# Slots of an expert dealt over the partitions, another order for one load back, and an earlier reload of x, in a two-layer decoder step

## The reference

```python
h = rmsnorm(x, norm_ffn[layer])
g_sel = argmax(h @ w_group + b_group)                 # one of 4 groups
top_v, top_i = top_k((h @ w_router + b_router)[g_sel], 2)   # two of its 8 experts
gates = softmax(top_v) * p_group
x = x + sum_over_the_two( gate * (silu(h @ w_gate[e]) * (h @ w_up[e])) @ w_down[e] )
```

```text
layer 0: 23 36 24 29 42 44 48 50 36 41 39 35 44 52 23 50 49 28 28 37 30 33 31 34 37 35 22 32 39 36 36 29
layer 1: 45 38 41 31 31 32 40 32 36 44 42 35 43 27 38 33 36 35 33 35 39 43 46 31 30 38 37 36 28 34 26 37
```

## Time and profile before

| | us |
|---|---|
| median of 3 runs | 1351.07 (1345.57 to 1353.43) |
| the profiled execution's own time | 1357.84 |
| its span in the profile | 1356.2 |
| PE busy (share of the span) | 1193.0 (88%) |
| DVE busy | 421.2 (31%) |
| ACT busy | 264.3 (19%) |
| POOL busy | 309.7 (23%) |
| mean granted TensorE clock | 0.944 |

### The profile page before, as it was taken

One profiled execution on the slowest core, in us unless ns is written; L12 is line 12 of the kernel. 1 busy time (PEld: TensorE's weight loads), 2 busy tenths in 40 slices (PEclk: granted clock), 3 DMA queues, 4 the chain that ended last, 5 costly groups with the idle time before them and its releaser, 6 DMA issues.

```text
span 1356.2 us, 16557 instructions
## 1 busy us (share of the span) xinstructions
PE 1193.0 (88%) x6257; PEld 626.1 (46%) x6257; DVE 421.2 (31%) x881; ACT 264.3 (19%) x627; POOL 309.7 (23%) x328
## 2 busy tenths in 40 slices
PE   7899999998899899887867999998899899887880
PEld 6655675565544433332324754446744533333320
DVE  6732116644303611111116601034602611111115
ACT  3111117743203001000013221125302100000001
POOL 2441403422000111111003241366710101111102
PEclk9989999999899999888988999998999799888995
DMA  9322308689776599999958220605456689999966
GB/s 299 106 54 88 132 0 268 208 321 367 281 302 274 201 408 421 420 420 420 413 215 307 83 67 0 202 0 172 138 185 274 230 335 422 420 421 420 418 246 217
DMA packets 105825, 344.99 MB, mean 254 GB/s; under 512 B 22638, under 2 KB 41010, under 8 KB 81930
## 3 DMA queue, kind: packets, MB, share of 16 engines
q1 hardware_dynamic: 91112, 307.96, 59.7%
q0 software_dynamic: 14336, 35.80, 7.3%
q10 hardware_dynamic: 290, 0.08, 0.0%
HBM read 324.81 MB, written 33.67 MB: 264 GB/s over the span
## 4 chain that ended last, share of the span: by engine, by line
PE 54%; SPq 16%; DMA 14%; DVE 8%; issue 3%; POOL 3%; ACT 1%; PEldq 1%; PEld 0%; POOLq 0%; DVEq 0%; ACTq 0%
SPq L1356 10%; PE ps L1566 8%; PE ps L2206 7%; PE ps L614 6%; PE ps L1491 6%; SPq L1378 5%; DMA moe_gu<-in_moe_w_up 4%; PE ps L610 4%; DMA fox_arena<-negs_rows 3%; DMA moe_wd<-in_moe_w_down 3%; PE ps L1584 3%; PE ps L2175 2%; PE ps L958 2%; DMA moe_gu<-expert_rows 2%; PE ps L970 2%
## 5 line engine op out<-in xcount | busy, mean ns | idle before, releaser
L1566 PE MATMUL ps<-moe_gu,rows 128*64 128x512 f32 x1024 | 247.9, 640 | 53.4 <-DMA moe_gu<-in_moe_w_up 50.8
L1566 PEld LDWEIGHTS ps<-moe_gu,rows 128*64 128x64 f32 x1024 | 81.0, 147 | 200.7 <-issue 192.1
L1450 POOL DMA_INDIRECT expert_rows<-turned,moe_row x32 | 32.1, 1002 | 391.8 <-ACT turned L1679 359.6
L1853 DVE TENSOR_TENSOR turned<-turned,ps 128x256 f32<-128x256 f32 x32 | 13.5, 422 | 306.3 <-ACT turned L1669 306.3
L1584 PE MATMUL ps<-moe_wd,moe_rowsel 128*64 128x512 f32 x352 | 80.4, 598 | 2.7 <-DMA moe_wd<-in_moe_w_down 2.7
L1669 ACT ACTIVATE turned<-ps 128x256 f32<-128x256 f32 x32 | 12.3, 383 | 304.3 <-PE ps L1566 304.3
L449 POOL TENSOR_TENSOR fox_arena<-fox_arena 128x512 f32<-128x512 f32 x32 | 45.5, 1440 | 65.6 <-PE ps L610 56.5
L614 PE MATMUL ps<-x,fox_arena 128*128 128x288 f32 x224 | 56.0, 406 | 0.0
L1443 POOL DMA_INDIRECT turned<-h_rows,moe_row x32 | 33.2, 1036 | 78.0 <-DVE moe_row L1812 43.0
L1858 DVE COPY turned<-ps 128x512 f32<-128x512 f32 x32 | 22.1, 692 | 86.8 <-PE ps L1584 86.8
L614 PE MATMUL ps<-turned,fox_arena 128*128 128x288 f32 x168 | 45.0, 422 | 3.6 <-DVE fox_arena L661 3.6
(11 more groups left out here) (426 smaller groups left out, 1920.9 us busy)
## 6 DMA issues: line engine op xcount, KB each, us to landing
moe_gu<-in_moe_w_gate SPq DMA_DIRECT2D x56, 1024.0 KB, 21.6
moe_gu<-in_moe_w_up SPq DMA_DIRECT2D x56, 1024.0 KB, 23.5
moe_wd<-in_moe_w_down SPq DMA_DIRECT2D x44, 1024.0 KB, 23.9
rows<-in_moe_w_down SPq DMA_DIRECT2D x20, 1024.0 KB, 22.6
fox_arena<-in_cache_v POOLq DMA_DIRECT2D x32, 512.0 KB, 12.5
fox_arena<-in_fox_w_in SPq DMA_DIRECT2D x6, 2048.0 KB, 10.0
fox_arena<-in_cache_k SPq DMA_DIRECT2D x20, 512.0 KB, 10.8
moe_gu<-in_moe_w_gate SPq DMA_DIRECT2D x16, 512.0 KB, 10.1
```

Source lines behind the costliest of these rows:

```text
L1566: mm = pe.matmul(ps[h, 2 + p % 2, :].rearrange("s (k f) -> s k f", k=2), xT[:, c, h], gu[s][:, half, :, c, :], start=(c == 0), stop=(c == ...
```

## The change

It has three parts: the constant `iota_slot`, the order of the load back in layer 0, and the place of the reload of `x`.

```diff
-    c["iota_slot"][:] = np.arange(SLOT)
+    c["iota_slot"][:] = np.arange(SLOT).reshape(PER, PER).T.reshape(-1)
...
             def late_(sp):
                 sp.wait_ge(scattered, 1)
-                for n in range(NT):
+                for n in range(NT) if layer else (0, 1, L, 2, 3):
                     sp.dma_start(held[n][0:ROWS[n], :], y_dram[2 * n * P:2 * (n * P + ROWS[n]), :].rearrange("(p j) d -> p (j d)", j=2)
                                  ).then_inc(back_in[layer][n], 16)
...
                     sp.dma_start(C[:, b, :, 0:MV], i["state_C"][0, b].rearrange("(p h) d v -> (h d) p v", h=2)).then_inc(c_in, 16)
+                sp.wait_ge(w_product, 24)
+                for n in range(NT):
+                    sp.dma_start(x[0:ROWS[n], n, :], x_dram[n * P:n * P + ROWS[n], :]).then_inc(x_again, 16)
                 sp.wait_ge(c_in, 16 * SB)
...
                         gate_rows_in(sp, tri[p], p, k, negg_dram, tri_in[p - 2])
-                for n in range(NT):
-                    sp.dma_start(x[0:ROWS[n], n, :], x_dram[n * P:n * P + ROWS[n], :]).then_inc(x_again, 16)
                 sp.wait_ge(cp_kept, 1)
```

## The result

The changed kernel takes 1358.82 us in the median of 12 runs (1353.87 to 1369.18), the kernel before 1352.73 us in 12 runs beside them (1345.57 to 1358.35). The ratio is 1.0049, 95% interval 1.0025 to 1.0073: 6.6 us slower (3.4 to 9.9), about 0.5%. The profiled execution took 1360.54 us, against 1357.84 before.

What follows compares the result with a forecast made beforehand. PE is mostly busy, but the weights' DMA sets the pace in both layers' experts. Terms +8.0 - 6.8 + 0 = +1.2 us on the median of 1351.07 gave 1352.3 us, range 1344 to 1361.

Steps and rivals of the forecast that it cites:

- Part 1, the assignment: Gathers and scatters: each DMA engine serves groups of four neighbouring partitions, partitions 32 to 35 back on the first engine.
- Part 1, the price: Ends of both expert phases: 64 more rows on the busiest engine at 0.125 us each, +8.0 us (+4.5 and +3.5).
- the upper end: Highest price of a row on the busiest engine, 0.16 us, read from layer 0's last scatter on idle queues.
- a longer tail: End of both expert phases: about eight engines busy to the end, share near 0.5, landing 4.5 and 3.5 us later.
- Part 2: Load back of layer 0: sample tile loaded third, so DVE's sums start at 731.6 instead of 738.37, -6.8 us.
- DVE's list: DVE's steps at the load back from 713.5: 10.8 us of additions and copies, last addition ending at 725.4.
- quicker flips: PE's second flip at the load back may run quicker after a shorter wait, worth up to 1 us.
- Part 3: Reload of x moved into an empty DMA queue in the phase before: 0, bounds -0.5 and +0.5 us.
- A: Expert phases: a row costs more when eight engines are full, 0.31 us, kernel at 1364 us; chance 0.12.
- decision point: Row price in the expert phases above which the dearer-row rival would hold: 0.21 us a row.
- B: Expert phases: engines served by blocks of eight, so dealing evens the rows, 18 us faster, 1326 us; chance 0.05.
- C: Expert phase ends: the late engine is late by nature, so dealt slots cost nothing, 1344.3 us; chance 0.09.

Runs made afterwards that it cites:

- e4_groups: Kernel before with slot ranks dealt over groups of four partitions, the groups that DMA engines serve: ratio 0.9917, 11.2 us faster.
- e1_deal: Kernel before with only the change's new `iota_slot`, slots dealt by eights: ratio 1.0108, 14.6 us slower.
- e5_one: Kernel before with ranks 0 to 7 of every expert on one group of four partitions in each half, the others dealt over seven groups: ratio 1.0079.
- e8_nogather: Kernel before with every gathered row's index out of bounds, so gathers are issued but move no row: ratio 0.9817, expert phases 228.3 and 227.9 us.
- e6_odd: Kernel before with the change's dealt slots mirrored, so the odd groups of four partitions hold the eight rows: ratio 1.0102.
- e2_late: Kernel before with only the load back of layer 0 reordered, sample tile third: ratio 0.9963, 5.0 us faster.
- e3_x: Kernel before with only the five reloads of x moved as in the change: ratio 0.9984, not told from no difference.
- e7_best: Changed kernel with slots dealt over groups of four partitions instead of by eights: 1333.9 us, ratio 0.9841 to the kernel before.

## Why the prediction was right, and where it was off

**The direction and the size of the whole.** Forecast: +1.2 us, within 0.5%. Measured: +6.6 us (3.4 to 9.9), at the very edge of what was called no change (6.8 us), inside the range. The interval leaves out zero: the change is slower. It came about as forecast, from two parts that work against each other, but the cancelling was less good than 8.0 against 6.8. That it stayed inside 0.5%, by 0.2 us, was in part luck: one of the two terms was off by 3.5 us.

**Part 1, the assignment.** Groups of four partitions, wrapping after 32, were read from the lone engine in the last scatter. The tails with a share of 0.51 for eight full engines and 0.13 for two, and the scatter at 0.50, bear it out. The Trainium skill states that rule for plain transfers ("DMA: Bandwidth & Descriptors", "The descriptor swizzle"); these runs agree with it for an indirect DMA as well.

**Part 1, the price: the term that was mis-sized.** It was put at 64 rows x 0.125 us = +8.0, by the lag of the last engine behind the mean one. The trace after has 237.99 us from the first gate product to scatter 14 (issued at 702.36) in layer 0 against 230.38, and 3.9 us more in layer 1: +11.5 us in all, 0.18 us for each of the forecast's 64 rows. Nearly all of the miss is in layer 0 (+7.6, forecast +4.5); layer 1's +3.9 was forecast as +3.5. Part 1 alone cost 14.6 us in the runs (11.4 to 18.0). The idle scatter's 0.16 us, which was called the upper end, is the better price: from e4_groups to e1_deal the busiest engine has 70 and 76 rows more, and the phases are 11.9 and 13.0 us longer, 0.17 us a row in both.

The step that failed was to take the price from the tails, and with it the forecast of a longer tail. The same measure in the changed kernel (layer 0, then layer 1), and in layer 0 of e5_one:

```profile
686.00:702.00 16.00, 11.14 (x50) 3.52 (x47) 1.26 (x3) 2.05 (x5) 1.00 (x1) 1.00 0.50 206
...
1306.00:1320.00 14.00, 9.90 (x44) 3.07 (x41) 1.11 (x2) 1.36 (x3) 0.98 (x1) 1.00 0.62 249
```

```profile
685.00:703.00 18.00, 14.62 (x60) 4.94 (x58) 1.80 (x3) 2.23 (x5) 1.00 (x1) 0.91 0.32 133
```

The mean engine ends at 686 + 0.50 x 16 = 694.0 and the last at 701.9, 7.9 us late; in layer 1 it is 1314.7 and 1319.9, 5.3 us late. Before, these lags were 7.5 and 8.1 us. So the lag hardly grew in layer 0 and shrank in layer 1, while the phases became longer: it is the mean engine that ends later, by 7.2 and 6.7 us against the phase's start, since engines already stand idle ahead of the tail. In e5_one, with a busiest engine as full and a phase as long, the lag is 10.1 us. The lag depends on how many engines are late, and doesn't price a row.

That isn't all: in layer 0 a row costs 0.12 to 0.14 us up to 178 rows (e8_nogather, e4_groups, before), and 0.17 to 0.21 from there to 214 or 216 (the changed kernel, e1_deal, e5_one, e6_odd); in layer 1 those kernels give 0.12 to 0.20 and e4_groups 0.18. Why layer 0 bends was not settled. Both theories of the price assumed a straight line.

**Part 2.** Forecast -6.8 us by DVE's list; the trace has 34.8 - 27.4 = 7.4 less, and e2_late 7.0. The list held step by step: last addition 21.85 us after the first issue by forecast, 21.8 in the trace (729.95 + 2.6 - 710.80). The remaining 0.6 us lie behind it, at PE's last flip. Before, then after:

```profile
734.08 2.11 PE L2245 MATMUL ps<-turned,mwblk 128*128 128x288 f32 x8
736.02 1.05 PE L2257 MATMUL ps<-cst,rows 128*128 128x128 f32 x8
```

```profile
735.76 1.16 PE L2260 MATMUL ps<-cst,rows 128*128 128x128 f32 x8 [1.26 <-ACT rows L2391]
```

Before, ACT had the last tile scaled at 735.29, and the flip waited 0.73 us behind products of PE, which had worked at half clock until about 733. After, it waits 0.05 us. The prediction had named quicker flips as worth up to 1 us. But e1_deal and e4_groups have no such wait either, and their last tile takes as long as in the changed kernel without part 2 (5.68 us from the last addition to the first sum), so these 0.6 us can't be put down to part 2 alone. In the runs part 2 alone shows 5.0 us (2.3 to 7.7).

**Part 3.** Forecast 0; e3_x can't be told from no difference, and POOL's wait stays (9.32 us in the changed kernel, 9.49 before).

**The sum.** By the runs of the single parts, +14.6 - 5.0 - 2.2 = +7.4 us, by the traces +11.5 - 7.4 = +4.1; the whole measured +6.6. Of the 5.4 us between forecast and result, 3.5 are thus the price of a row, and part 2 takes 0.6 off again. The 2.5 us left over are within what the runs can tell: executions of one kernel differ by 10 us or so. Much of it lies ahead of the experts, where these kernels are the same up to their constants: the first gate product comes at 456.9 in e2_late and at 469.0 in e8_nogather.

**The rivals.** A (dearer rows because eight engines are full) was right that a row can cost more, 0.20 us in layer 0 against its decision point of 0.21. Its cause is not borne out by e5_one, on the strength of layer 0 alone. B and C fell by e1_deal and e4_groups, and e6_odd shows no slower engine in the odd half.

## What to carry to other kernels

When all DMA engines are busy and a wait ends with a transfer, look at the last microseconds before it: a share that falls in steps means that single engines are behind, and the sum of bytes no longer tells the time. Count what each engine carries and spread the uneven part (rows that are only sometimes there) over the groups that the engines serve; spreading it by another pattern can pile it up, as here. Take the price of such a row from two kernels that differ in it, not from how far the last engine lags behind the mean. Load first what is needed first: where two orders meet, as here at the load back, the second one's order decides.

## What was not expected of the hardware

Two full engines of 16 delay a phase as much as eight do (245.4 and 245.6 us against 246.0 and 245.9), though in one case the rate of the whole falls to 53 GB/s at the end and in the other to 205. And before, the granted clock fell from 1.00 to 0.50 while PE idled for 6.30 us ahead of its second flip, and stayed there from 724 to 732; the changed kernel has 1.00 in that stretch. In all seven traces without part 2, the second flip comes after 6.3 to 7.5 us of idling and takes 1.97 us; in the three with it, it takes 1.06 to 1.16. A shorter pause can stand ahead of a slow flip too: in e7_best it is the first flip that takes 1.97 us, after 2.27 us of idling, with the granted clock at 0.50 from 709.5 to 711.5. Little of this reaches the first sum, which comes 28.2 us after the load back's first issue in e7_best and 27.4 in the changed kernel.
